# Second feed-forward's down projection: six feature tiles as plain products, sixteen by a seven-product scheme with products of 256 tokens

## The reference

```python
hn = rmsnorm(h, pre_ffn_norm[i])
ff = (jax.nn.silu(hn @ w_gate[i]) * (hn @ w_up[i])) @ w_down[i]
h = h + rmsnorm(ff, post_ffn_norm[i])
e = rmsnorm(p[i] @ w_ple_proj[i], ple_norm[i])
gate = jax.nn.sigmoid(h @ w_ple_gate[i] + b_ple_gate[i])
h = h + e * gate
```

## Time and profile before

| | |
|---|---|
| runs | 1526.61, 1527.83, 1528.1 us (median 1527.83) |
| span of the profiled execution | 1525.5 us |
| its own time | not listed apart; it is one of the same program, the runs lie 1.1 to 2.6 above its span |
| PE busy | 1511.5 us (99%) |
| DVE, ACT, POOL busy | 1136.2, 799.4, 149.6 us |
| granted TensorE clock, mean | 0.999 |

### The profile page before, as it was taken

The page is one execution under the profiler, slowest core; times in us unless marked ns, Lnnn a source line. Parts: engine busy times, 40 slices in busy tenths (PEclk is TensorE's granted clock), DMA queues, the critical chain, the costliest instruction groups (busy, mean ns, idle before and its releaser), DMA issues.

```text
span 1525.5 us, 21551 instructions
## 1 busy us (share of the span) xinstructions
PE 1511.5 (99%) x8214; PEld 1290.1 (85%) x8214; DVE 1136.2 (74%) x1844; ACT 799.4 (52%) x1284; POOL 149.6 (10%) x158
## 2 busy tenths in 40 slices
PE   8999999999999999999999999999999999999998
PEld 3788877878888899999888888788888999988887
DVE  8999988897898789977664547766577888843356
ACT  5545467764553656666442335446355666643233
POOL 0111000000000101111011011110202111100100
PEclk9999999999999999999999999999999999999999
DMA  9778221223566547666633323211234566573241
GB/s 370 184 187 202 83 90 62 88 86 108 210 230 211 165 117 190 197 162 166 184 100 103 111 86 100 75 49 42 97 116 147 147 165 164 145 250 101 87 138 69
DMA packets 66632, 213.05 MB, mean 140 GB/s; under 512 B 7773, under 2 KB 10077, under 8 KB 65506
## 3 DMA queue, kind: packets, MB, share of 16 engines
q1 hardware_dynamic: 52784, 178.63, 34.3%
q0 software_dynamic: 13744, 33.04, 11.2%
q10 hardware_dynamic: 2, 0.00, 0.0%
HBM read 175.47 MB, written 7.87 MB: 120 GB/s over the span
## 4 chain that ended last, share of the span: by engine, by line
PE 91%; DVE 4%; ACT 2%; issue 1%; DMA 1%; ACTq 0%; DVEq 0%; SPq 0%
PE bank L1940 18%; PE bank L1941 18%; PE bank L1948 18%; PE bank L1978 8%; PE bank L1988 8%; PE bank L1980 8%; PE bank L2006 2%; PE bank L2020 1%; PE bank L2018 1%; PE bank L2019 1%; PE bank L2110 1%; PE bank L2093 1%; PE bank L2123 1%; DVE tmp L2670 1%; PE bank L2137 1%
## 5 line engine op out<-in xcount | busy, mean ns | idle before, releaser
L1940 PE MATMUL bank<-HH,sph 128*128 128x512 f32 x856 | 342.9, 401 | 2.2 <-ACT xpad L2227 0.8
L1941 PE MATMUL bank<-HH,spl 128*128 128x512 f32 x856 | 333.9, 390 | 0.0
L2537 DVE TENSOR_TENSOR spl<-raw,sph 128x1024 fp32r<-128x1024 f32 (+2 forms) x166 | 205.2, 1238 | 161.4 <-ACT sph L2168 161.3
L2168 ACT ACTIVATE sph<-raw 128x1024 fp32r<-128x1024 f32 (+2 forms) x186 | 189.1, 1020 | 150.8 <-PE bank L1948 117.5
L1948 PE MATMUL bank<-HL,sph 128*128 128x512 f32 x856 | 225.5, 396 | 0.0
L1940 PEld LDWEIGHTS bank<-HH,sph 128*128 128x128 f32 x856 | 160.8, 188 | 40.1 <-issue 5.7
L1941 PEld LDWEIGHTS bank<-HH,spl 128*128 128x128 f32 x856 | 160.8, 188 | 34.5 <-issue 1.4
L1948 PEld LDWEIGHTS bank<-HL,sph 128*128 128x128 f32 x856 | 159.8, 188 | 35.2 <-issue 1.9
L2599 DVE SCALAR_TENSOR_TENSOR convout<-convin,vecs,convout 128x512 f32<-128x512 f32 x240 | 166.4, 748 | 0.0
L1978 PE MATMUL bank<-HH,sph 128*128 128x256 f32 x576 | 144.7, 284 | 0.0
L1980 PE MATMUL bank<-HH,spl 128*128 128x256 f32 x576 | 144.4, 283 | 0.0
(11 more groups left out here) (366 smaller groups left out, 2686.4 us busy)
## 6 DMA issues: line engine op xcount, KB each, us to landing
raw<-in_w_in SPq DMA_DIRECT2D x69, 512.0 KB, 3.2
raw<-in_w_up SPq DMA_DIRECT2D x66, 512.0 KB, 4.5
more<-in_w_ada SPq DMA_DIRECT2D x32, 512.0 KB, 5.6
raw<-in_w_down SPq DMA_DIRECT2D x32, 512.0 KB, 3.7
raw<-in_w_gate SPq DMA_DIRECT2D x22, 512.0 KB, 3.8
raw<-raw POOLq DMA_DIRECT2D x36, 256.0 KB, 4.4
midl<-tmp POOLq DMA_DIRECT2D x36, 256.0 KB, 3.3
spl<-raw POOLq DMA_DIRECT2D x17, 512.0 KB, 5.5
```

The source lines that it names most:

```text
L1940: e.matmul(P_[b][:], sph(n)[:, q], hi[:, k, :], start=k == 0, stop=False)
L1941: e.matmul(P_[b][:], spl(n)[:, q], hi[:, k, :], start=False, stop=False)
L2168: e.activation(sph(n), raw(n), ACT.Copy).then_inc(*up("s_w_high", ("wh", n)))
L2537: e.tensor_tensor(spl(n), raw(n), sph(n).bitcast(F32), ALU.subtract).then_inc(*up("s_w_low", ("wl", n)))
```

## The change

The last sixteen hidden tiles (6 to 21) are kept whole in `midf` after `seven_mid`, and rounded from there. The down projection does tiles 0 to 5 first for all eight outputs, in units of 768 weight columns, and ACT copies each bank into `XT` (`down_plain`). Then four pairs of output tiles are done by the seven-product scheme over tiles 6 to 21: 28 products of 8 feature tiles by 256 tokens, 24 matmuls each. The activation sums `ds` (`down_t_sum`), their high and low parts (`dh`, `dl`) are made during the plain tiles, the weight sums by DVE (`down_sum`, in `bsum` and `sums`) and a POOL DMA (`down_third`). Of the units z0 to z3 of a pair, z2 goes into a buffer of its own (`extra`). After a product DVE adds or subtracts its bank to `XT` (`down_add`); the squares follow once a tile is whole. The residual is reloaded into `FFO` instead of `XT`, late (`x_reload` at steps 23 and 24), and the gain is applied in the join. The six embedding squares are made in place and added up apart (`e_square`, `e_total`, `e_join`). The host permutes the rows of `w_down`.

```diff
+DOWN_PLAIN = 6
+DOWN_PARTS = 28
+DOWN_FIRST = ((6, 14), (10, 18))
...
+    def down_factors(st, count, beside=None):
+        while st["made"] < min(count, st["total"]):
+            s = st["made"]
+            pos = s % 7
+            if pos in (2, 3):
+                add("down_sum", s)
+            add("down_high", s)
+            if beside:
+                beside()
+                beside = None
+            add("down_low", s)
+            st["made"] += 1
+            if pos in (2, 4, 5) or pos == 6 and s < st["total"] - 1:
+                load()
+            if pos == 6 and s < st["total"] - 1:
+                add("down_sum", s + 2)
+                add("down_third", s // 7 + 1)
+        if beside:
+            beside()
...
-    sse = SumSq("e")
-
-    def e_sum():
-        for i in range(6):
-            sse.add(("EC", i), [("e_copy",)])
-            yield
...
+    def t_sums(t):
+        for g in range(2):
+            add("down_t_sum", t, g, [label for j in range(4) for label in frees[j]] if t == 3 else [])
+        for g in range(2):
+            add("down_t_high", t, g)
+
+    def down_first():
+        t_sums(0)
+        yield
+        t_sums(1)
+        yield
+        add("down_t_low", 0, 0)
+        yield
+        add("down_t_low", 0, 1)
+        yield
+        t_sums(3)
+        yield
+        add("down_t_low", 1, 0)
+        add("down_t_low", 1, 1)
+        yield
+        for g in range(2):
+            add("down_x_low", 0, g)
+        yield
+        for g in range(2):
+            add("down_t_sum", 2, g, [])
+        yield
+        add("down_sum", 1)
+        add("down_third", 0)
...
+    lo_engine[0] = "dma"
+    load()
+    side.append(down_first())
+    rate[0] = 1
     for i in range(8):
-        if i == 1:
+        gemm("w_down", i, DOWN_PLAIN, "m2", plain_evac(i))
+    flush()
+    rate[0] = 0
+    lo_engine[0] = "dve"
+    assert W["used"] == n_down
+    for p in range(4):
+        units.extend([("w_down", 2 * p, 768, 1024), ("w_down", 2 * p + 1, 768, 1024),
+                      ("w_down", 2 * p + 1, 1792, 1024), ("w_down", 2 * p, 1792, 1024)])
+        W["used"] += 4
+    banks = [main.take() for _ in range(4)]
...
+    def down_settle(s):
+        p, pos = divmod(s, 7)
+        b = banks[2 + p % 2 if pos in (1, 5) else p % 2][0]
+        if pos != 3:
+            add("down_add", p, pos, b)
...
+    for s in range(DOWN_PARTS):
+        if s == 1:
             add("e_copy")
-            side.append(e_sum())
-            rate[0] = 1
             add("p_load", 2)
-        if i == 7:
-            flush()
-            rate[0] = 0
+            ssf = SumSq("ff")
+        down_factors(down, s + 3, lambda: down_settle(s - 1) if s else None)
+        if s:
+            down_square(s - 1)
+        W["cut"] = max(W["cut"], down["first"] + down["made"])
+        if s < 2:
+            add("down_t_high", 2, s)
+        if 1 <= s < 3:
+            add("down_t_low", 2, s - 1)
+        if s in range(8, 20, 2):
+            add("e_square", (s - 8) // 2)
+        if s in range(11, 21, 2):
+            add("e_total", (s - 9) // 2)
+        if s == 22:
+            add("p_cut", 2)
             add("root_table", keepc(1))
-            add("p_cut", 2)
-        gemm("w_down", i, NFT, "m2", branch("FFO", i, ssf), 2 if i == 7 else 1)
+        if s >= DOWN_PARTS - 2:
+            split()
+        if s in (23, 24):
+            add("x_reload", 2, s - 23)
+        add("down", s, banks[s // 7 % 2], banks[2 + s // 7 % 2])
+        done()
+    down_settle(DOWN_PARTS - 1)
+    down_square(DOWN_PARTS - 1)
...
+            def down(s, sums, pairs):
+                p, pos = divmod(s, 7)
+                step = step_of(s)
+                whole_sum, pair = P_[sums[0]][:, 0:256], P_[pairs[0]]
+                to = {1: pair[:, 0:256], 3: pair[:, 256:512], 4: pair[:, 256:512]}.get(step, whole_sum)
+                begins = step in (0, 1, 3)
+                if step == 0:
+                    w.wait_ge(*(each(sums[1]) if p < 2 else [at("down_add", p - 2, 6)]))
+                elif step == 3:
+                    w.wait_ge(*(each(pairs[1]) if p < 2 else [at("down_add", p - 2, 5)]))
+                elif step == 2:
+                    w.wait_ge(at("down_add", p, 0))
+                elif step == 4:
+                    w.wait_ge(at("down_add", p, 1))
+                elif step == 5:
+                    w.wait_ge(at("down_add", p, 2))
+                elif step == 6:
+                    w.wait_ge(at("down_add", p, 4))
+                w.wait_ge(at("down_low", s))
...
+            p, z = divmod(n - n_down, 4)
+            s = 7 * p
+            return [[("down_low", s), ("down_sum", s + 2), ("down_third", p)],
+                    [("down_sum", s + 1), ("down_low", s + 4)],
+                    [("down_sum", s + 1), ("down_low", s + 6)],
+                    [("down_sum", s + 3), ("down_low", s + 5)]][z]
...
+                if n == fourth[1]:
+                    w.wait_ge(*[at("down_low", 7 * p + 6) for p in (2, 3)])
...
+            def down_plain(i, b, g):
+                w.wait_ge(at("tile", g), *fenced("d2"))
+                e.activation(XT[:, i, :], P_[b][:], ACT.Copy).then_inc(*up("s_branch_a", ("down_plain", i)))
+
+            def down_t_high(t, g):
+                w.wait_ge(at("down_t_sum", t, g), *fenced("d2"))
+                if t == 2:
+                    w.wait_ge(at("unit", n_down - 1))
+                e.activation(DH[t][g], DS[t][g], ACT.Copy).then_inc(*up("s_cut_a", ("down_t_high", t, g)))
+
+            def down_high(s):
+                given, after = down_given(s)
+                w.wait_ge(at(*down_free(s)), *each(after))
+                e.activation(SPH[down_slot(s)][:], given, ACT.Copy).then_inc(*up("s_w_high", ("down_high", s)))
...
+                if whole_mid(which, f):
+                    q = slice(0, 256 if any(first <= f < first + 4 for first in DOWN_FIRST[0]) else 512)
+                    e.activation(MH[:, f, q], MF[:, f, q], ACT.Copy).then_inc(*up("s_cut_a", ("hi", "m2", f)))
+                    return
...
+            def down_add(p, pos, b):
+                i = 2 * p + (pos in (1, 4, 6))
+                cols = {0: slice(0, 256), 5: slice(0, 512), 6: slice(0, 256)}.get(pos, slice(256, 512))
+                bank = P_[b][:, 256:512] if pos == 1 else P_[b][:] if pos == 5 else P_[b][:, 0:256]
+                w.wait_ge(at("down", 7 * p + pos), at("down_plain", i))
+                before = {2: [], 4: [1], 5: [0, 2]}.get(pos, [])
+                w.wait_ge(*[at("down_add", p, z) for z in before])
+                last = {5: [("ff", i)], 6: [("ff", i)]}.get(pos, [])
+                e.tensor_tensor(XT[:, i, cols], XT[:, i, cols], bank, ALU.subtract if i % 2 else ALU.add).then_inc(
+                    *up("s_branch", ("down_add", p, pos), *last))
...
+                    e.scalar_tensor_tensor(TMP[j][:], XT[:, i, :], vec("g_pof", i), P_[b][:], ALU.mult,
+                                           ALU.mult).then_inc(*up("s_x", ("join", name, i)))
+                    w.wait_ge(at("join", name, i), at("x_back", 2, i // 4))
+                    e.tensor_tensor(XT[:, i, :], FFO[:, i, :], TMP[j][:], ALU.add).then_inc(
...
+            def down_third(p):
+                n = n_down + 4 * p
+                w.wait_ge(at("raw", n), at("raw", n + 1), at("down_sum", 7 * p + 1))
+                e.dma_start(raw(n + 1), raw(n), accum_op=ALU.add).then_inc(
+                    *G.up(f"d_down{p % 2}", ("down_third", p), by=16))
```

More of the change, by code:

```diff
@@ L1474, in ffn_rows @@
             add("seven_full", 2, i)
-    sse = SumSq("e")
-    def e_sum():
-        for i in range(6):
-            sse.add(("EC", i), [("e_copy",)])
-            yield
     ffn_up(2, "n4", lambda i, z: (("w_gate", "w_up")[z], i), ffn_rows)
     fence("d2")
-    ssf = SumSq("ff")
-    for i in range(8):
-        if i == 1:
+    ssf = None
+    frees = dict(tmp.take() for _ in range(NT))
+    for j in range(4, NT):
+        tmp.give(j, *frees[j])
+    n_down = W["used"] + 8
+    down = {"first": n_down + sum(st["slots"] - st["units"] for st in stages), "units": 16, "slots": DOWN_PARTS,
+            "total": DOWN_PARTS, "made": 0, "down": True}
```

300 lines of the change are left out of this document (249 added, 51 removed).

## The result

The changed kernel takes **1537.32 us** (median of 4 runs, 1537.0 to 1537.67) against 1527.49 for the kernel before in the same series: ratio 1.0066, 95% interval 1.0053 to 1.008. It is slower by about 10 us; 1529.1 was forecast, with a range up to 1534.5. The profiled span is 1535.9 us, 10.4 more than before.

The account below looks back on a forecast made before the run. The prediction took TensorE (PE), busy 99% of the span, to bound the kernel. Its terms, -6.5 + 3.8 + 2.2 + 1.8 = +1.3, gave a span of 1526.8 us and runs of about 1529.1, range 1524.0 to 1534.5.

Parts of the forecast that it names:

- Term 1: PE's work in the down projection: 113.3 us of matmuls instead of 119.87, -6.5 us if PE never waits.
- Term 2: Plain tiles: PE waits at d2 and d3 for accumulating DMAs landing in 4.0 us; +3.8 us (3.1 to 5.3).
- d4, d5 and d6 come in time: Plain tiles: these units' low parts are ready after 6.7 us, against 8.2 available, so PE does not wait.
- Term 3: Plain tiles: d7's DMA stands behind the first `down_third` on POOL's queue, so PE waits; +2.2 us (0 to 5).
- z1's buffer is free only when d5's DMA has landed: ... 22.3: Plain tiles: the step timing z1's load, at 22.3 us after d0's start, ahead of `down_sum(1)` and `down_third`.
- hardly any load runs then: Plain tiles: the reason for taking 4.0 us as the landing of a 384 KB accumulating DMA.
- a rival with 0.08: DVE slips in the products (+1) or the clock falls in a wait: about 1533 to 1535 us, chance 0.08.
- I cost all of this at nothing: Products: DVE's work and the tight `down_add` waits cost 0; if DVE slips, 0 to +1 us.
- Term 4: Tail: ACT's root comes 3.65 us after the last product's end against 1.98, and a longer join; +1.8 us (0.5; 2.5).
- POOL's two subtractions come in time: Tail: POOL's low parts are ready for the gate matmuls, which are shifted by as much as the tail grows.

Follow-up runs that it names:

- third_behind_d7: Against the changed kernel, the first `down_third` stands behind d7's accumulating DMA on POOL's queue instead of ahead of it; 1534.02 us.
- loads_held: As sum_behind_lows, but z1's load and all later loads wait until d7's accumulating DMA has landed; 1533.5 us.
- embedding_work_spread: Against the changed kernel, the `e` squares, `e` additions and `ptl` subtractions are put at other products; 1537.35 us.
- sum_behind_lows: Against the changed kernel, DVE makes six lows of x and t before `down_sum(1)`, with `down_third(0)` following it, behind d7's DMA; 1533.15 us.
- plain_lows_by_dve: Against the changed kernel, DVE subtractions make the low parts of d2 to d7, instead of ACT's negated copy and POOL's accumulating DMA; 1532.43 us.
- mixed_lows: On sum_behind_lows, DVE makes the lows of d2, d3 and d7, d4 to d6 keep DMAs, two t roundings go behind d3's cut; 1529.75 us.

## Why the prediction was wrong

Its sum was +1.3; the spans differ by 10.4. Right was the direction of each term, wrong the size of three; the products had been costed at nothing, and the fall of the clock stood only in a rival.

- **Term 1** (-6.5): right. Plain units without waits take 4.08 each, a product 2.875.
- **Term 2** (+3.8): right at d2 and d3 (1.76 and 1.97 for 1.8 and 2.0). The landing, taken as 4.0, was 3.8 for both, and the first DMA went 0.3 later than I had it; that the two made up for each other at d2 is luck. "d4, d5 and d6 come in time" failed for d5 (+0.54), whose DMA took 6.2 us; with small gaps at three others the term is 4.5.
- **Term 3** (+2.2, measured 5.15): the failed step is "z1's buffer is free only when d5's DMA has landed: ... 22.3". That DMA took 6.2 instead of 4.0, and z1's load could go only at 24.7. The loads of z1 and z2 then took until 30.0 instead of 26.4, and d7's DMA went at 32.3 instead of 28.2. It landed in 5.8, about as forecast (6.2), and PE wanted it 0.8 later than I had it. The mechanism (POOL's queue) was right, and third_behind_d7 shows it. I had argued that "hardly any load runs then"; beside d5's DMA a load ran for 4.2 us, a second for 0.9, and d6's DMA for the last 1.8. That loads and DMAs beside it lengthen a landing is shown for d7's DMA by loads_held (3.8 against 8.4); for d5's no run takes them away, and d6's landed in 4.1 though two loads began about 2 us into it. Why d5's took 6.2 stays open.
- **The clock** (+2.0): only in a rival with 0.08. That rival's price for a unit at half speed, 4.1, was twice too much, because the clock was back within the unit; its time, 1533 to 1535, was the nearest of all and still too low, for it counted on the same small terms 3 and 4.
- **The products** (0, measured +2.0): the failed step is "I cost all of this at nothing". The wait on the `down_add` of the product two before, which I named as the tightest, with 0.1 to 0.2 us to spare, came twice, 1.0 us each by starts, with an `e` addition or the cut of `ptl` in DVE's queue. I had counted the `e` squares on ACT and forgotten that their additions are DVE's. embedding_work_spread took away half; the wait that stayed has only DVE's chain ahead of it, with 0.85 us of waiting for ACT's rounding, which I had not counted.
- **Term 4** (+1.8, measured +3.3): the root's time was right to 0.13 (3.52 for 3.65). The failed step is "POOL's two subtractions come in time": I asked only when they end, not what DVE does meanwhile. The second one holds the join's operation until its own end; that operation ends 4.5 us after the root instead of 2.7 before, 1.4 of it by its own length and 0.4 by a later start at half the clock.

Together: 0.7 + 2.95 + 2.0 + 2.0 + 1.5 more than the terms had, 9.15 of the 9.1 that were missing.

## What to carry to other kernels

When a low part moves from a DVE subtraction to a copy and a DMA, price the DMA's landing beside the loads and other DMAs of that very stretch, and count every buffer that comes free only with that landing: a late landing delays the loads, and these the next landing. Ask of a POOL operation not only whether it ends in time, but which DVE operations with two SBUF inputs it falls upon. And when waits in a row are taken away, the next unit with the same chain takes them over, as d4 did from d2 and d3: take the whole chain off, and then look at the engine that took its work (here DVE, behind which some 2 us stay), and at what that engine itself waits for.

## What the runs showed of the hardware

- The accumulating DMA of 384 KB within SBUF landed in 3.8 to 4.1 us with little beside it. Beside three loads of 512 KB and, towards its end, an accumulating DMA of 512 KB it landed in 7.6 (third_behind_d7) and 8.4 (sum_behind_lows); the loads took 4.3 to 5.6 in the first and up to 8.2 in the second, instead of about 3.1. The Trainium skill ("DMA: Bandwidth & Descriptors", "Anatomy of one DMA — SWDGE (gpsimd) path") gives an estimated 2.9 by its fit; no run here came under 3.8.
- The clock fell with a short wait too. It fell in the wait of 4.99 us, and in plain_lows_by_dve it was down from about 1395.4 on, when PE had been busy again for 1.5 us after a wait of 1.79. After waits of 2.27 (mixed_lows) and 2.74 us (sum_behind_lows) it stayed at 1.00. What tells these apart stays open. In d7's unit the fall cost 1.8 to 2.9 us (5.99 to 7.05 us in four runs, 4.20 with the wait filled). In the tail it cost nothing where PE waits for the join (8.97 and 8.98 with and without), but in embedding_work_spread, where the clock was 0.50 from 1478.33 to 1485.15 and PE was busy up to the first gate matmul, the tail took 9.33.
